# One score matrix in the first scan, attention tiles in pairs, and narrow products prepared ahead, in a two-block kernel on one core

## The chip, the core and the metric

The kernel runs on one core of a Trainium2 chip. The metric is the device time of one execution in microseconds; 2547.91 us is the median of three runs of the kernel before (2546.81 to 2548.03). The engines are TensorE (PE in the profile; PEld is its weight load), VectorE (DVE), ScalarE (ACT), GpSimd (POOL) and SyncE (SP), which issues the large loads. Each works through a queue of its own; they meet in counting semaphores.

## What is computed

Two blocks follow each other on 256 latent tokens of width 1024.

The first block has two layers on 256 latent and 256 context tokens (512 in all):

```python
h = modulate(x, norm1_g[i], shift, scale)          # both streams; shift, scale, gates = silu(c) @ ada_w + ada_b
o = gla_mixer(h) if i == 0 else na_mixer(h)        # gated linear attention, then neighbourhood attention
x = x + g1 * o
x = x + g2 * conv_ffn(modulate(x, norm2_g[i], ...))
```

`gla_mixer`: 4 heads, forward and backward direction, chunks of 64 tokens. In each direction a token attends to itself and to the earlier (later) ones of its chunk with decay, and takes the state of the chunks before. Both directions are added, normalised per head, multiplied by silu(r), transposed and projected. `na_mixer`: 16 heads of 64; 256 latent queries against 512 keys, softmax of scores + bias, times values. `conv_ffn`: two products to 2816 columns (one through a three-tap convolution and silu), their product, and a narrow product back to 1024. The second layer ends with the latent stream only.

The second block is a convolution and scan mixer and a mixture of 64 experts over 256 tokens, whose 400 MB of weights are read whole. The change touches nothing in it.

## The kernel before

The first block keeps activations transposed (features on partitions, 8 chunks of 128). Products of activations with weights are split: weight and activation are each rounded (`..._hi`, on ScalarE) and the rest taken (`..._lo`, on VectorE), and `split_mm` (L519) makes three fp32r products. All large weights come as 88 slabs through four ring slots, issued by SyncE in one fixed order, each when the product that used its slot last is done (`free`); the experts' weights follow in the same queue.

The order on each engine is written out by hand: one function per engine (`@block.tensor`, `scalar`, `vector`, `gpsimd`, `sync`).

First scan (L670 to L745). A step `hd` is one head and direction (even forward, odd backward). On TensorE: `scan_scores` (scores of all chunks into bank 0), `scan_keys` (four transposes, bank 1), `gate_logits(hd + 2)`, `late_turn(hd - 1)`, `scan_updates(hd, 0)`, `late_rows(hd, 0)`, in odd steps from 3 on `y_turn`, `scan_updates(hd, 1)`, the rest of `late_rows`, in odd steps `scan_out`. `late_rows` multiplies a 2 MB slab of the modulation weights each, two or three slabs a step (`ADA_BATCH`); they fill time of the scan. `late_read` (ScalarE) copies the rows, `late_turn` brings the bias and the rows into columns, `late_columns` (ScalarE) stores them. On VectorE a step is `decayed(hd + 1)`, `mask_scores` (predicated copy of bank 0 into `g_att[dr]`), every second time `gated`, `states(hd)` (seven steps of 64x256 to 128x256, the first four behind update 0, the rest behind update 1), `cumulate(hd + 2)`. On ScalarE: `keys_turned`, `late_columns`, `gate_log(hd + 2)`, `y_turned`, `decays(hd + 2)`, `late_read`, `scan_norm`; in step 0 also SiLU over `g_r`. `scan_out(h)` adds, for each of four token tiles, two products of the score matrices with v and up to four with states. Then the projection: six of eight chunks of the first four column groups, `y_turn` of the last head, and the rest with residual and norm sums (L744 to L762).

Feed-forward (`ffn` on each engine). 22 wide units, each of two products of 8 chunks; unit 21 ends the wide part. Then `wo_hi` and `f_lo`: ScalarE rounds the first narrow slab (`ffn_w_out_hi(l, 0)`) and all 22 activation chunks (`f_hi`), VectorE takes the rests. TensorE's eight narrow groups of 22 chunks wait for all of `ffn_act`, for `w_lo` and, in the first group, for each `f_lo`.

Attention (L798 to L834). A tile `i` is one head and 128 queries (h = i // 2). TensorE: scores of tile i + 2, transposes of tile i (four), output of tile i - 1 (four products of 64 columns out). VectorE: score + bias (L2009), maximum (L2011), its negation (L2012), and for the tile before reciprocal and scaling (L2018, L2019). ScalarE: exponential with sum, copy of the transposed tile, copy of the output. Three tiles `n_s`, three score banks. GpSimd waits for the last value product, loads `metaT`, clears `n_bias` and then loads the 32 bias tiles, four ahead.

## Time and profile before

| | us |
|---|---|
| median of 3 runs | 2547.91 |
| the profiled execution | 2554.06 |
| its span, first to last instruction | 2551.8 |
| TensorE busy | 2097.3 (82%) |
| VectorE busy | 912.5 (36%) |
| ScalarE busy | 673.3 (26%) |
| GpSimd busy | 56.0 (2%) |

| stage | from | to |
|---|---|---|
| first modulation slabs, first projections | 0 | 195 |
| first scan | 195 | 341 |
| its projection and norm | 341 | 420 |
| first feed-forward, wide / narrow | 420 / 674 | 669 / 804 |
| q, k, v products of the attention | 814 | 934 |
| attention | 934 | 1037 |
| projection, second feed-forward | 1037 | 1275 |
| second block up to the experts | 1275 | 1600 |
| experts and end | 1600 | 2552 |

A timeline row gives start, length, engine and line, and in brackets how long the engine had been idle before it and what ended that. A single fp32 product has two records on PE (a transpose one), so counts are twice the products; some records are missing. PEclk in the stretch table is the clock granted to TensorE, 1.00 being 2.4 GHz and 0.50 1.2 GHz.

### The profile page before, as it was taken

The numbers are of one execution on the slowest core, as the hardware profiler recorded it, in microseconds if no ns is written. First come the engines' busy times: TensorE is split into PE (matmuls) and PEld (weight loads), VectorE is DVE, ScalarE is ACT, GpSimd is POOL, SyncE is SP. The second block draws the span as 40 slices with busy tenths as digits, with TensorE's granted clock in tenths as the row PEclk, the third lists the DMA queues.
The fourth block names the chain that finished last, engine by engine and source line by source line (L and its number), as shares of the span: only waits on it lengthen the run. The fifth ranks groups of instructions, "written<-read, shape, count | busy, mean of one in ns | idle before, by whom it ended". The sixth has DMA issues, their size and how long they took to land.

```text
span 2551.8 us, 37428 instructions
## 1 busy us (share of the span) xinstructions
PE 2097.3 (82%) x16374; PEld 1521.8 (60%) x16374; DVE 912.5 (36%) x1638; ACT 673.3 (26%) x1173; POOL 56.0 (2%) x81
## 2 busy tenths in 40 slices
PE   6997998999998989999989999666666666666655
PEld 4895755888776875799988445433343343334332
DVE  2335623433423217466475432433311111111112
ACT  4234313323314315455355211111111111111111
POOL 0011100000000011000010000000000000000000
PEclk9998899999998989999999998788888888878888
DMA  7107741222222321153541035599999999999996
GB/s 318 67 34 302 293 179 52 99 99 79 69 101 99 118 98 48 69 184 139 190 168 42 1 155 198 244 426 428 426 427 427 427 425 428 427 427 427 427 427 288
DMA packets 44433, 592.11 MB, mean 232 GB/s; under 512 B 5528, under 2 KB 5717, under 8 KB 8176
## 3 DMA queue, kind: packets, MB, share of 16 engines
q1 hardware_dynamic: 40608, 579.36, 55.5%
q0 software_dynamic: 2880, 8.45, 1.0%
q8 instruction: 131, 2.15, 0.3%
q10 hardware_dynamic: 784, 1.91, 0.2%
q14 instruction: 30, 0.25, 0.0%
HBM read 588.64 MB, written 1.05 MB: 231 GB/s over the span
## 4 chain that ended last, share of the span: by engine, by line
PE 54%; DMA 26%; DVE 4%; ACT 2%; issue 1%; POOL 0%; DVEq 0%; ACTq 0%
DMA s_ring<-in_w_up 10%; PE bank L521 10%; PE bank L523 10%; PE bank L522 10%; DMA s_arena<-in_w_up 8%; PE bank L1091 5%; DMA s_xT<-in_w_up 4%; DMA s_hT<-in_w_up 3%; PE bank L1105 2%; PE bank L1004 1%; PE bank L813 1%; PE bank L803 1%; PE bank L941 1%; PE bank L758 1%; DMA s_arena<-in_w_down 1%
## 5 line engine op out<-in xcount | busy, mean ns | idle before, releaser
L521 PE MATMUL bank<-s_arena_r 128*128 128x256 f32 (+2 forms) x1656 | 544.1, 329 | 36.9 <-DVE s_hT_r L1788 34.5
L1212 ACT ACTIVATE s_arena<-bank 32x256 f32<-32x256 f32 (+6 forms) x455 | 180.1, 403 | 1105.7 <-PE bank L1091 573.6
L523 PE MATMUL bank<-s_arena_r,s_ring_r 128*128 128x512 f32 (+2 forms) x1312 | 442.3, 337 | 0.0
L1091 PE MATMUL bank<-s_ring,s_arena 128*32 128x256 f32 x2048 | 301.3, 506 | 135.8 <-DMA s_xT<-in_w_up 45.7
L522 PE MATMUL bank<-s_hT_r,s_arena_r 128*128 128x512 f32 (+2 forms) x1096 | 369.8, 337 | 0.0
L521 PEld LDWEIGHTS bank<-s_arena_r 128*128 128x128 f32 x1656 | 314.3, 190 | 73.0 <-issue 33.3
L1783 DVE TENSOR_TENSOR s_ring_r<-s_ring,s_arena_r 128x2048 fp32r<-128x2048 f32 (+1 forms) x96 | 232.5, 2425 | 301.6 <-ACT s_arena_r L1212 301.5
L1091 PEld LDWEIGHTS bank<-s_ring,s_arena 128*32 128x32 f32 x2048 | 145.4, 144 | 216.2 <-issue 203.0
L523 PEld LDWEIGHTS bank<-s_arena_r,s_ring_r 128*128 128x128 f32 x1312 | 251.5, 192 | 27.1
L1212 ACT ACTIVATE s_arena_r<-s_ring 128x2048 fp32r<-128x2048 f32 (+1 forms) x96 | 193.2, 2016 | 139.2 <-PE bank L523 138.1
L522 PEld LDWEIGHTS bank<-s_hT_r,s_arena_r 128*128 128x128 f32 x1096 | 210.8, 192 | 21.7
L2331 DVE TENSOR_TENSOR s_arena<-s_arena,bank 64x256 f32<-64x256 f32 x64 | 27.1, 423 | 545.1 <-ACT s_arena L1212 545.1
L1091 PE MATMUL bank<-s_arena 128*32 128x256 f32 x1024 | 128.9, 510 | 83.4 <-DMA s_ring<-in_w_up 36.0
L1091 PEld LDWEIGHTS bank<-s_arena 128*32 128x32 f32 x1024 | 66.2, 145 | 121.0 <-issue 114.5
L1212 ACT ACTIVATE s_arena<-s_arena 128x512 f32<-128x512 f32 (+7 forms) x182 | 92.6, 542 | 166.3 <-DVE s_arena L1776 78.3
L522 PE MATMUL bank<-s_ring_r,s_arena_r 128*128 128x256 f32 (+1 forms) x464 | 130.1, 280 | 0.0
L1091 PE MATMUL bank<-s_xT,s_arena 128*32 128x256 f32 x512 | 91.9, 537 | 37.3 <-DMA s_ring<-in_w_up 37.3
L522 PE MATMUL bank<-s_arena_r 128*128 128x512 f32 (+1 forms) x352 | 120.6, 343 | 0.0
L2387 DVE COPY s_arena<-bank 32x256 f32<-32x256 f32 x128 | 54.3, 424 | 143.4 <-PE bank L1105 141.0
L1091 PE MATMUL bank<-s_hT,s_arena 128*32 128x256 f32 x512 | 84.3, 501 | 16.3 <-DMA s_ring<-in_w_up 16.3
L523 PE MATMUL bank<-s_arena_r,s_hT_r 128*128 128x256 f32 (+1 forms) x336 | 94.3, 281 | 0.0
L1212 ACT ACTIVATE s_arena<-bank,s_cols 128x512 f32<-128x512 f32 (+2 forms) x76 | 48.5, 648 | 161.1 <-PE bank L523 123.7
(318 smaller groups left out, 2795.7 us busy)
## 6 DMA issues: line engine op xcount, KB each, us to landing
s_ring<-in_slabs SPq DMA_DIRECT2D x72, 2048.0 KB, 8.3
s_ring<-in_w_down SPq DMA_DIRECT2D x32, 2048.0 KB, 28.7
s_ring<-in_w_up SPq DMA_DIRECT2D x32, 2048.0 KB, 33.1
s_ring<-in_w_gate SPq DMA_DIRECT2D x32, 2048.0 KB, 33.4
s_arena<-in_w_gate SPq DMA_DIRECT2D x16, 2048.0 KB, 33.1
s_arena<-in_w_up SPq DMA_DIRECT2D x16, 2048.0 KB, 33.9
s_arena<-in_w_down SPq DMA_DIRECT2D x16, 2048.0 KB, 28.7
s_ring<-in_slabs SPq DMA_DIRECT2D x16, 1408.0 KB, 6.3
```

The costliest lines, as they stand in the source:

```text
L521: mm(out, w_hi_, x_hi_, start=start, stop=False)
L522: mm(out, w_hi_, x_lo_, start=False, stop=False)
L523: return mm(out, w_lo_, x_hi_, start=False, stop=stop)
L758: last = mm(pb[m % 4][:, :], w[:, k, 128 * (m % 4):128 * (m % 4) + 128], g_qk[:, 4 * (k % 2) + k // 2, :], start=k == 0, stop=k == DC - 1, ...
L803: mm(NA_BANK[i % 3][:, :], n_q[p0:p0 + 64, h // 2, 128 * qt:128 * qt + 128], n_k[p0:p0 + 64, h // 2, :], start=True, stop=True)\
L813: last = mm(pb[4 + i % 2][p0:p0 + 64, 0:128], n_v[:, k, 64 * h:64 * h + 64], n_pt[:, i % 2, 128 * k:128 * k + 128], start=k == 0, stop=k == 3)
L1091: last = mm(pb[b][32 * q:32 * q + 32, 0:256], x[:, c, :], w[q // 2][:, c, 256 * (q % 2):256 * (q % 2) + 256], start=c == 0, stop=c == DC - ...
L1105: last = mm(pb[3 + b][32 * q:32 * q + 32, 0:256], e_hT[:, b, 64 * a + 32 * half_:64 * a + 32 * half_ + 32], w[:, 2 * half_ + a, 256 * q:25 ...
L1212: return act.activation(out, in_, func, **kw)
L1783: TTn(view_r, view, hi.bitcast(F32), ALU.subtract).then_inc(S["w_lo"], 1)
L2331: return TTn(e_hid[0:64, b, :], e_sg[0:64, b, :], pb[b][64:128, 0:256], ALU.mult)
L2387: dve.tensor_copy(y_g[32 * j:32 * j + 32, g % 2, 256 * q:256 * q + 256], pb[3 + b][32 * q:32 * q + 32, 0:256]).then_inc(S["y_dve"], 1)
```

## The change

- Scan: one matrix `g_att` for both directions. The backward mask leaves the diagonal out; after the backward copy the matrix is multiplied by `g_twice` (2 on the diagonal, 1 elsewhere). `scan_out` makes one score product for each token tile.
- `r` is read from PSUM with SiLU in the same instruction; its second half goes to banks 4 to 7. `scan_scores(0)` waits for four of these reads, and the gate product of step 0 for all eight.
- `late_turn` is made of plain transposes, `late_columns` moves to VectorE (in `states`, before the fifth one) and adds the bias there; `late_read(hd - 1)` comes right after `keys_turned(hd)`. In each step from 1 on `scan_updates(hd, 0)` comes before `late_turn`, and all `late_rows` after the second update.
- Projection behind the scan: five groups ahead instead of four, the last turn after the first and the last y transposes after the third of them.
- Feed-forwards: before unit 21's own work ScalarE rounds the first narrow slab and chunks 0 and 1, VectorE takes their rests; these two have places of their own (`f_hi`). TensorE waits for 20 activations instead of 22, and the narrow groups use banks 2 to 5.
- Attention: tiles in pairs of heads (`na_tile`): tile 2j on partitions 0 to 63, tile 2j + 1 on 64 to 127. Scores come as two products one after the other into two of four banks, outputs as eight products in turn on the two halves of one bank, with one copy. Six logit tiles. Scores are negated while the bias is taken off, the minimum is the bias of an exponential with scale -1. The scores of pairs 0 and 1 are made between the value products, pair 2 right behind, and ScalarE's first four exponentials between its value copies. GpSimd loads metaT and the bias from the end of the first feed-forward on.

```diff
+        n_s = [n_s01[:, 0, :], n_s01[:, 1, :], n_s23[:, 0, :], n_s23[:, 1, :], sq[:, 0, :], sq[:, 1, :]]
+
+        def na_tile(i):
+
+            return 2 * (i // 4) + i % 2, i // 2 % 2
...
-            pool.wait_ge(S["na_v_mm"], 16)
+            pool.wait_ge(S["ffn_out_mm"], DC)
...
+                pool.dma_start(n_bias[:, i % 4, 0:NT], d["na_bias"][h, qt]).then_inc(S[f"na_bias_in{i % 4}"], 16)
...
-                pe.wait_ge(S["ffn_act"], 22 * l + FC)
+                pe.wait_ge(S["ffn_act"], 22 * l + FC - 2)
...
             def late_turn(b):
                 pe.wait_ge(S["ada_row"], ADA_EARLY + b + 1)
-                k, (l, s) = ADA_BATCH[b], divmod(ADA_AT[b], ADA_N)
-                mm(pb[5][:, 3 * P:3 * P + 8 * k], ident, col("ada_b2", 96 * l + 8 * s, 8 * k), start=True, stop=False, skip_group_check=True)
-                for i in range(k):
-                    o = 3 * P + 8 * i
-                    last = mm(pb[5][:, o:o + 8].rearrange("p (j n) -> p j n", n=2), ada_late_sb[:, i, :], ada_sel, start=False, stop=True, skip_group_check=True)
+                for i in range(ADA_BATCH[b]):
+                    last = pe.transpose(pb[5][:, P * i:P * i + P], ada_late_sb[:, i, :], ident)
                 last.then_inc(S["ada_tr"], 1)
...
-                    for dr in range(2):
-                        mm(bank[:, o:o + 256], g_att[:, dr, P * tt:P * tt + P], g_v[:, tt, 256 * h:256 * h + 256], start=dr == 0, stop=False,
-                           skip_group_check=True)
+                    mm(bank[:, o:o + 256], g_att[:, P * tt:P * tt + P], g_v[:, tt, 256 * h:256 * h + 256], start=True, stop=False, skip_group_check=True)
...
                 scan_scores(hd)
                 scan_keys(hd)
+                if hd == 0:
+                    pe.wait_ge(S["gla_r_ev"], 8)
...
                     gate_logits(hd + 2)
+                scan_updates(hd, 0)
                 if hd >= 1:
                     late_turn(hd - 1)
-                scan_updates(hd, 0)
-                late_rows(hd, 0)
+                else:
+                    late_rows(hd, 0)
                 if hd >= 3 and hd % 2:
                     y_turn(hd // 2 - 1)
                 scan_updates(hd, 1)
-                for i in range(1, ADA_BATCH[hd]):
+                for i in range(0 if hd else 1, ADA_BATCH[hd]):
                     late_rows(hd, i)
                 if hd % 2:
                     scan_out(hd // 2)
-            late_turn(7)
-            w = got(FIRST["gla_out"])
-            for m in range(4):
+            for m in range(GLA_AHEAD):
+                w = got(FIRST["gla_out"] + m // 4)
                 for k in range(6):
-                    mm(pb[m][:, :], w[:, k, 128 * m:128 * m + 128], g_qk[:, 4 * (k % 2) + k // 2, :], start=k == 0, stop=False, skip_group_check=True)
-            y_turn(HEADS - 1)
+                    mm(pb[m][:, :], w[:, k, 128 * (m % 4):128 * (m % 4) + 128], g_qk[:, 4 * (k % 2) + k // 2, :], start=k == 0, stop=False,
+                       skip_group_check=True)
+                if m == 0:
+                    late_turn(7)
+                if m == 2:
+                    y_turn(HEADS - 1)
             pe.wait_ge(S["gla_y_ev"], 2 * HEADS)
...
+            def na_scores(j):
+                for a in range(2):
+                    i = 2 * j + a
+                    h, qt = na_tile(i)
+                    if i >= 4:
+                        pe.wait_ge(S["na_add"], i - 3)
+                    mm(NA_BANK[i % 4][:, :], n_q[64 * a:64 * a + 64, h // 2, 128 * qt:128 * qt + 128], n_k[64 * a:64 * a + 64, h // 2, :],
+                       start=True, stop=True).then_inc(S["na_s_mm"], 1)
+
+            def na_out(j):
+                pe.wait_ge(S["na_pt"], 2 * j + 2)
+                if j >= 2:
+                    pe.wait_ge(S["na_o_ev"], j - 1)
+                for k in range(4):
+                    for a in range(2):
+                        i = 2 * j + a
+                        h, qt = na_tile(i)
+                        last = mm(pb[j % 2][64 * a:64 * a + 64, 0:128], n_v[:, k, 64 * h:64 * h + 64], n_pt[:, i % 4, 128 * k:128 * k + 128],
+                                  start=k == 0, stop=k == 3, skip_group_check=True)
+                last.then_inc(S["na_o_mm"], 1)
...
+                if k in (8, 9):
+                    na_scores(k - 8)
+            na_scores(2)
...
+            for j in range(NA_H):
+                for a in range(2):
+                    i = 2 * j + a
+                    pe.wait_ge(S["na_p"], i + 1)
+                    if i >= 2:
+                        pe.wait_ge(S["na_pt"], i - 1)
+                    for k in range(4):
+                        last = pe.transpose(pb[2 + a][:, 128 * k:128 * k + 128], n_s[i % 6][:, 128 * k:128 * k + 128], ident)
+                    last.then_inc(S["na_tr"], 1)
+                if j >= 1:
+                    na_out(j - 1)
+                if j + 3 < NA_H:
+                    na_scores(j + 3)
...
-                ffn_w_out_hi(l, 0)
                 act.wait_ge(S["ffn_in_mm"], 44 * (l + 1))
-                act.wait_ge(S["ffn_act"], 22 * (l + 1))
-                for c in range(FC):
+                for c in range(2, FC):
+                    act.wait_ge(S["ffn_act"], 22 * l + (c + 1 if c < DC + 2 else FC))
                     A(f_hi(c, T), f_act[:, c, 0:T], ACT.Copy).then_inc(S["f_hi"], 1)
...
+                    if i == FC - 1:
+                        ffn_w_out_hi(l, 0)
+                        for c in range(2):
+                            A(f_hi(c, T), f_act[:, c, 0:T], ACT.Copy).then_inc(S["f_hi"], 1)
...
-                    copy("gla_r_mm", 8 * s + 4 + u + 1, "gla_r_ev", pb[u][:, :], g_r[:, u, 512 * s:512 * s + 512])
+                    copy("gla_r_mm", 8 * s + 4 + u + 1, "gla_r_ev", pb[4 * s + u][:, :], g_r[:, u, 512 * s:512 * s + 512], func=ACT.Silu)
...
+            r_read(0)
             r_read(1)
+            tables(LOG_EXP)
             for hd in range(8):
                 keys_turned(hd)
                 if hd >= 1:
-                    late_columns(hd - 1)
+                    late_read(hd - 1)
                 if hd + 2 < 8:
...
-                if hd == 0:
-                    act.wait_ge(S["gla_r_ev"], 8)
-                    for u in range(4):
-                        A(g_r[:, u, :], g_r[:, u, :], ACT.Silu).then_inc(S["gla_r_ev"], 1)
-                late_read(hd)
...
+            late_read(7)
...
-                A(n_s[:, i % 3, :], n_s[:, i % 3, :], ACT.Exp, bias=n_mx[:, i % 3, 1:2], accum_out=n_rs[:, i % 3, 0:1]).then_inc(S["na_exp"], 1)
...
+                A(n_s[i % 6], n_s[i % 6], ACT.Exp, scale=-1.0, bias=n_mx[:, i % 6, 0:1], accum_out=n_rs[:, i % 6, 0:1]).then_inc(S["na_exp"], 1)
+
+            def na_read(j):
+                act.wait_ge(S["na_o_mm"], j + 1)
+                h, qt = na_tile(2 * j)
+                A(n_o[:, h // 2, 128 * qt:128 * qt + 128], pb[j % 2][:, 0:128], ACT.Copy).then_inc(S["na_o_ev"], 1)
+            for k in (10, 11):
+                half_hi(k, "na", NA_DONE)
+            for u in range(8):
+                if u >= 4:
+                    na_exp(u - 4)
+                copy("na_v_mm", 8 * (u // 4) + 4 + u % 4 + 1, "na_v_ev", pb[u % 4][:, :], n_v[:, u % 4, 512 * (u // 4):512 * (u // 4) + 512])
...
+                if i % 2 == 0 and i >= 2:
+                    for a in range(2):
+                        if i + 2 + a < 2 * NA_H:
+                            na_exp(i + 2 + a)
...
+                if i >= 2 and i % 2 == 0:
+                    na_read(i // 2 - 1)
+            na_read(NA_H - 1)
...
+                def act_rest(c):
+                    dve.wait_ge(S["f_hi"], FC * l + c + 1)
+                    TTn(f_lo[:, c, 0:T], f_act[:, c, 0:T], f_hi(c, T).bitcast(F32), ALU.subtract).then_inc(S["f_lo"], 1)
...
+                    if i == FC - 1:
+                        ffn_w_out_lo(l, 0)
+                        for c in range(2):
+                            act_rest(c)
...
-                ffn_w_out_lo(l, 0)
-                for c in range(FC):
-                    dve.wait_ge(S["f_hi"], FC * l + c + 1)
-                    TTn(f_lo[:, c, 0:T], f_act[:, c, 0:T], f_hi(c, T).bitcast(F32), ALU.subtract).then_inc(S["f_lo"], 1)
+                for c in range(2, FC):
+                    act_rest(c)
...
+                att = g_att.rearrange("p (a n) -> p a n", n=P)
+                if dr:
+                    dve.wait_ge(S["att_cp"], hd)
+                last = dve.copy_predicated(att, in_chunk[dr].bitcast(U32).unsqueeze(1).to_broadcast([P, 4, P]), pb[0][:, :].rearrange("p (a n) -> p a n", n=P))
+                if dr:
+                    step(last)
+                    last = TTn(att, att, g_twice.unsqueeze(1).to_broadcast([P, 4, P]), ALU.mult)
+                last.then_inc(S["att_cp"], 1)
...
+            def late_columns(b):
+                k, (l, s) = ADA_BATCH[b], divmod(ADA_AT[b], ADA_N)
+                dve.wait_ge(S["ada_tr"], ADA_EARLY + b + 1)
+                TTn(mod[:, l, 4 * s:4 * s + 4 * k, :], pb[5][:, 0:P * k].rearrange("p (j n) -> p j n", n=32)[:, :, 0:2],
+                    col("ada_b2", 96 * l + 8 * s, 8 * k).rearrange("p (j n) -> p j n", n=2), ALU.add).then_inc(S["ada_late"], 1)
...
+                    if i == 4 and hd >= 1:
+                        late_columns(hd - 1)
...
-                TTn(n_s[:, i % 3, :], NA_BANK[i % 3][:, :], n_bias[:, i % 4, :], ALU.add).then_inc(S["na_add"], 1)
+                if i >= 6:
+                    dve.wait_ge(S["na_tr"], i - 5)
+                STT(out=n_s[i % 6], in0=NA_BANK[i % 4][:, :], scalar=-1.0, in1=n_bias[:, i % 4, :], op0=ALU.mult, op1=ALU.subtract).then_inc(S["na_add"], 1)
...
-                step(dve.tensor_reduce(n_mx[:, i % 3, 0:1], n_s[:, i % 3, :], AX_X, ALU.max))
-                TS(n_mx[:, i % 3, 1:2], n_mx[:, i % 3, 0:1], -1.0, None, ALU.mult).then_inc(S["na_max"], 1)
...
+                dve.tensor_reduce(n_mx[:, i % 6, 0:1], n_s[i % 6], AX_X, ALU.min).then_inc(S["na_max"], 1)
...
+            for k in range(1, 11):
+                half_lo(k, "na")
+            for i in range(2):
+                na_add(i)
+            half_lo(11, "na")
+            for i in range(2, 4):
+                na_add(i)
+            for j in range(NA_H):
+                for a in range(2):
+                    na_share(2 * j + a)
+                if j + 2 < NA_H:
+                    for a in range(2):
+                        na_add(2 * j + 4 + a)
```

## Rows read from the trace of the kernel before

**Rows 1.** Stretch table: us; busy PE, PEld, DVE, ACT, POOL; PEclk, DMA share, GB/s
```profile
1700.00:2500.00 800.00, 522.11 (x5828) 304.55 (x5820) 168.79 (x454) 86.83 (x243) 0.00 (x0) 0.83 1.01 427
```

**Rows 2.** Timeline of PE in the scan: start us, us, engine, line, instruction, count
```profile
227.62 1.13 PE L713 MATMUL bank<-s_arena 128*128 128x256 f32 x4
...
239.00 0.40 PE L598 MATMUL bank<-s_cols,s_ka 128*128 128x24 f32 x2
...
239.99 1.13 PE L702 MATMUL bank<-s_arena 64*128 64x256 f32 x8
```

**Rows 3.** Waits of PE in 195:341: waited for, us in total, times, longest
```profile
PE bank L598 <- ACT s_arena L1212: 15.0, 3, 9.1
PE bank L702 <- DVE s_arena L1943: 0.8, 3, 0.3
```

**Rows 4.** Timeline of ACT in steps 0 and 1 of the scan
```profile
208.71 2.91 ACT L1212 ACTIVATE s_arena<-s_arena 128x512 f32<-128x512 f32 x7 [8.54 <-DVE s_arena L1908]
...
212.93 3.90 ACT L1212 ACTIVATE s_ring<-s_ring 128x1024 f32<-128x1024 f32 x4
```

**Rows 5.** Stretch table in the scan and at the first narrow group
```profile
280.00:285.00 5.00, 5.00 (x99) 4.23 (x95) 2.35 (x6) 0.73 (x2) 0.00 (x0) 0.69 0.31 59
...
673.60:680.00 6.40, 6.35 (x17) 5.04 (x18) 6.40 (x11) 6.40 (x14) 0.00 (x0) 0.58 0.15 58
```

**Rows 6.** Timeline of PE in the projection behind the scan
```profile
364.40 3.70 PE L758 MATMUL bank<-s_arena,s_ring 128*128 128x512 f32 x8 [1.36 <-ACT s_arena L1212]
372.18 2.07 PE L506 MATMUL bank<-s_sq,s_ones 128*128 128x512 f32 x2 [4.08 <-ACT s_sq L1212]
```

**Rows 7.** Timelines at the joint of the first feed-forward: PE, DVE, ACT
```profile
673.65 0.76 PE L521 MATMUL bank<-s_hT_r,s_arena_r 128*128 128x512 f32 x1 [4.55 <-DVE s_arena_r L1820]
...
664.36 0.75 DVE L1775 SCALAR_TENSOR_TENSOR s_arena<-bank,s_cols,s_arena 128x510 f32<-128x510 f32 x1 [5.64 <-ACT s_arena L1212]
...
669.99 4.27 ACT L1212 ACTIVATE s_hT_r<-s_arena 128x512 fp32r<-128x512 f32 x8 [0.98 <-DVE s_arena L1816]
...
691.71 2.56 ACT L1212 ACTIVATE s_arena_r<-s_ring 128x2816 fp32r<-128x2816 f32 x1 [7.72 <-PE bank L523]
```

**Rows 8.** Timelines at the joint of the second feed-forward: ACT, DVE
```profile
1208.93 2.54 ACT L1212 ACTIVATE s_arena_r<-s_ring 128x2816 fp32r<-128x2816 f32 x1
...
1212.71 3.09 DVE L1783 TENSOR_TENSOR s_ring_r<-s_ring,s_arena_r 128x2816 fp32r<-128x2816 f32 x1
```

**Rows 9.** Timeline of PE in the attention: its start, and one tile
```profile
946.77 1.11 PE L825 MATMUL bank<-s_ka,s_arena 128*128 128x128 f32 x4 [10.23 <-DVE s_arena L2019]
...
963.58 0.66 PE L825 MATMUL bank<-s_ka,s_arena 128*128 128x128 f32 x4
964.16 1.09 PE L813 MATMUL bank<-s_arena 128*64 128x128 f32 x8
965.18 1.12 PE L803 MATMUL bank<-s_arena 64*128 64x512 f32 x2
```

**Rows 10.** Stretch table in the attention
```profile
946.80:962.00 15.20, 15.20 (x44) 8.71 (x45) 8.17 (x20) 5.21 (x14) 2.15 (x4) 0.50 0.10 32
962.00:1034.00 72.00, 71.32 (x381) 42.17 (x379) 54.95 (x133) 44.02 (x108) 11.82 (x22) 1.00 0.15 43
```

**Rows 11.** Timelines at the start of the attention: POOL, DVE
```profile
937.40 2.16 POOL L463 DMA_DIRECT2D s_arena<-in_na_bias  x4 [0.31 <-POOL s_arena L458]
...
943.00 0.69 DVE L2009 TENSOR_TENSOR s_arena<-bank,s_arena 128x512 f32<-128x512 f32 x1 [38.70 <-DMA s_arena<-in_na_bias]
...
946.04 0.15 DVE L2018 RECIPROCAL s_arena<-s_arena 128x1 f32<-128x1 f32 x1
...
946.63 0.68 DVE L2009 TENSOR_TENSOR s_arena<-bank,s_arena 128x512 f32<-128x512 f32 x1
```

**Rows 12.** Timeline of PE in the second block's scan: 64-column outputs in alternating halves
```profile
1413.67 0.66 PE L922 MATMUL bank<-s_arena 128*64 128x128 f32 x8
1414.26 0.71 PE L918 MATMUL bank<-s_arena 128*128 128x128 f32 x4
```

More of the change, by code:

```diff
@@ L634, in _, with token_major @@
             pe.wait_ge(S["gla_qk_ev"], 8)
-            def token_major(k, name, freed, after):
+            def token_major(k, name, freed, after, first=0):
                 wh, wl = g_w_hi[k % 2 + (2 if k >= 8 else 0)], half(place_r[FIRST["gla"] + k // 2], k % 2)
@@ L685, in scan_keys @@
                     pe.wait_ge(S["kd_cp"], hd)
-                else:
-                    pe.wait_ge(S["gla_r_ev"], 8)
                 pe.wait_ge(S["late_decayed"], 2 * hd + 2)
@@ L754, in _ @@
                 w = got(FIRST["gla_out"] + m // 4)
-                if m >= 4:
-                    pe.wait_ge(S["proj_x"], 2 * (m - 3))
-                for k in range(6 if m < 4 else 0, DC):
-                    last = mm(pb[m % 4][:, :], w[:, k, 128 * (m % 4):128 * (m % 4) + 128], g_qk[:, 4 * (k % 2) + k // 2, :], start=k == 0, stop=k == DC - 1,
+                if m >= GLA_AHEAD:
+                    pe.wait_ge(S["proj_x"], 2 * (m - GLA_AHEAD + 1))
+                for k in range(6 if m < GLA_AHEAD else 0, DC):
+                    last = mm(pb[m % GLA_AHEAD][:, :], w[:, k, 128 * (m % 4):128 * (m % 4) + 128], g_qk[:, 4 * (k % 2) + k // 2, :], start=k == 0, stop=k == DC - 1,
                               skip_group_check=True)
@@ L1999, in _ @@
                 h_rest(2, c, hT[:, c, :], hT_r[:, c, :], h_hi[:, c, :])
-            for k in range(1, 12):
-                half_lo(k, "na")
             def na_add(i):
```

120 lines of the change are left out of this document (35 added, 85 removed).

## Prediction

> **What bounds the kernel now.** I read the stretch table first. From 1700 to 2500 us the 16 DMA engines are full at 427 GB/s [rows 1]: the expert stage, bound by its weights. Nothing in the diff touches it, and its loads stand in SyncE's queue behind semaphores of the work before it, so time won before it moves it forward whole. The change lies in four places ahead of it: the first scan (195 to 341 us) with the projection behind it (to 413), the joint between wide and narrow products in each feed-forward (669 and 1200), and the attention (934 to 1037). There I looked in the order of time for rows in which TensorE sat idle, and for what ended them; where it isn't idle, only an instruction less helps.
>
> **1. The scan and the projection after it.** TensorE's scan work is one queue, so an instruction less counts in full, as long as the chain beside it (states on VectorE, decays on ScalarE, turned keys) doesn't end later.
> - One score matrix: the two products of a token tile take 1.13, or 1.06 without what overlaps the next [rows 2], 0.53 each; 16 of 32 go: -8.5. The price, a 128x512 multiply of 0.69 (as L2009, [rows 11]) in each backward head, stands on VectorE ahead of the states, while the updates they need are still to come: 0, and without that cover +2.8.
> - Late columns: the bias product and three selections take 239.00 to 239.99 [rows 2]; four transposes take 0.58 [rows 9], three 0.45. About 0.5 for each of seven turns in the scan: -3.5.
> - SiLU moved ahead: in head 1 TensorE waits 9.1 for ScalarE [rows 3], which ends its decays at 211.6, loads a table and runs four SiLUs to 216.8 before its copies [rows 4]. The SiLUs now replace the copies of r from PSUM, under the projection. What ends last then is the key copy (0.6) behind the decays, at 212.2; the wait runs from 208.0 to 212.3: -4.9. The table load held ScalarE for 1.3 (211.6 to 212.93, [rows 4]). The Trainium skill ("ScalarE: Activation LUTs", What ACT_TABLE_LOAD costs) counts 2.66 us for a switch of sets; by it this gain would be an estimated 1.4 larger, but the next ACTIVATE started after 1.3.
> - Updates no longer stand behind the turn, and all slabs of a batch follow the second update. In heads 3 and 5 the wait of 2.95 ((15.0 - 9.1) / 2, [rows 3]) falls to about 1.4, since one slab more (1.9) lies between the update that starts the chain and the wait, and the key copy (0.6) ends it and not the slab copy: -3.1. Heads 6 and 7 have no gate product left as cover: +1.9.
> - New waits: 2.15 us of states lie between the two updates, today covered by a slab's products (wait 0.3, [rows 3]). Now only the turn (0.3 to 0.45) stands there, in heads 3, 5, 7 also 1.0 of y transposes. Seven waits, of 1.35 to 1.7 and of 0.5 to 0.7, 7.8 in all, less 0.8 of today: +7.0.
> Sum -11.1. The clock: it is 0.69 at 280 to 285 [rows 5], behind a stretch without any wait, of 16-row and 8-column products and transposes. Two long waits go with the slow stretch behind them (-3); the new short waits thin the sparse stretches, and a dip can fall on any head: +1 to +8, I take +4. Scan -10.1 (-4 to -15). Slabs: 4.9 us each at 427 GB/s, three in 15, against heads of 12 to 19; one wait of 1, within this range.
> - Projection: TensorE waits 1.36 for the y copies and 4.08 for a square, which stands behind both engines' splitting of the next weights, and then runs at half clock (2.07 for a chunk of 1.02) [rows 6]. From the transposes' end (363.0) to the square 9.1 us pass. Now two groups of 5.2 (364.4's eight records are four products in 3.5, so 0.87 each, six a group) stand between: -7.6 with the turn's 0.45 (-5.6 if 2 us stick out).
> Together -17.7.
>
> **2. First feed-forward.** TensorE stops 4.55 [rows 7] for the split of the first narrow weights (2.54, 3.09, [rows 8]) and of the activations. Its first group runs from 673.65 to 691.71 (when ScalarE's wait for it ends), 18.05, of which 6.4 at a mean clock of 0.58 [rows 5]: 2.7 lost, 15.4 of work. Now the weight split (released when unit 20 ends, about 658) and chunks 0 and 1 lie under unit 21, whose convolution wants VectorE at 664.4 and gets it at 664.9; its result waits for 669.1 anyway. TensorE goes on at 669.1, waits 0.2 at chunk 2 and ends at 684.7. The second weight: ScalarE 20 x 0.53 from 669.1, then 2.54, makes 682.3; VectorE's 3.09 end at 685.3. The second group starts at 685.3 instead of 691.7: -6.4 (-4 if the clock dips there all the same).
>
> **3. Second feed-forward.** A unit lasts only 5.7 us, too short for 2.54 + 3.09. VectorE takes the last convolution only at 1201.3, the last SiLU ends at 1202.8, and ScalarE, then with 20 chunks, is at the second weight at 1208.9, as today [rows 8]. VectorE ends its part at 1214.6 instead of 1215.8, and the second group starts at least as much earlier, 1.2. But TensorE, done with the first group at 1210.7, waits 3.9 there and may pay 1.7 of half clock: -1 (-2 to +1).
>
> **4. Attention.** Start: TensorE idles 10.23 [rows 9], because the bias is asked for after the last value product: GpSimd issues from 937.40, the first sum starts at 943.00 [rows 11]. The loads now go out when the first feed-forward ends (GpSimd has nothing else queued between), and four tiles pass sum, maximum and exponential under the value products. After the stall TensorE is at clock 0.50 for 15.2 us [rows 10]; that goes too.
> Steady state: a tile takes TensorE transposes 0.58, outputs 1.02, scores 1.05 (1.12 less overlap), 2.65 in all, without a gap [rows 9]. A pair: scores 1.06, both halves of the rows at once (four 64-row products of 256 columns take 1.06 in [rows 2], 0.27 each, against 0.53 with 128 rows); transposes 1.16; outputs 16 records at the pace of 64-column outputs in alternating halves (eight in 0.59, [rows 12]): 1.18, or 2.04 if they don't overlap. Sum 3.4. VectorE: sum and negation in one operation, 0.75 (as L1775, PSUM and a scalar column, [rows 7]) + 0.03; minimum 0.62 (a pass over the same tile, priced as the sum's 0.69 of [rows 11] less overlap); reciprocal and scaling 0.59 (946.04 to 946.63, [rows 11]): 1.99 a tile, 3.98 a pair. ScalarE: exponentials 2 x 0.8, copies 2 x 0.53, 0.3: 3.0. VectorE becomes the bound, at 3.98 against 5.3.
> Time: the value products end at 933.9 and now carry two score pairs, 936.0; a third, 937.1. Thirteen periods and the last two sums (2.8) end at 991.7. Behind them scalings, transposes, outputs and copies of two pairs, no longer overlapped, 8.7: the projection starts at 1000.4 instead of 1036.9: -36.5. Bounds: outputs 1.5 a pair, -35.5; scores not overlapped, -27.5; fused sum 0.87, -33; 1.9 a tile, -39.
>
> **Sum.** -17.7 - 6.4 - 1 - 36.5 = -61.6. The profiled execution took 2554.06 (span 2551.8), 6.2 over the median of 2547.9: from its own time 2492.5, from the median 2486.3.
>
> **Rivals.** A: the halves don't overlap in the attention. TensorE needs 2.1 + 1.16 + 2.04 = 5.3 a pair as today, and only the start is won, -14.6: 2508. For it: no attention product has been issued this way; against it the two rows above. B: the clock. Every pair gets a wait of 0.6, and transposes are a third of the rest. At 1.2 GHz a pair costs 6.8, 16 pairs 109 us, 13 more than today instead of 36.5 less: 2535. Against it: 962 to 1034 ran at 1.00 with transposes a fifth of the time; for it, TensorE was busy for 15 us at 0.50 before that [rows 10]. The Trainium skill ("TensorE: Matmul & The Clock Gate", Part 4: PE-mode transpose) says that transposes don't count as busy for the clock, which speaks for B. C, slower: the same in the scan too, whose new waits follow updates and transposes. Its work is about 118 us, and what of it runs at half clock costs its own length again. On top of B the change loses from 12.5 us of it on; with a third of it (40) the time is 2575.
>
> **Chances.** Forecast 0.84, A 0.08, B 0.04, C 0.04. The parts' bounds give -40 to -70 for the forecast, 2478 to 2508, which takes A in; below I leave 4 more for clock dips outside the scan that may go too: 2474 to 2508. A measurement here tells 0.2% (5 us) from no change. Faster 0.95 (A and B with it), same 0.01 (C just past its point, or a part that I have not seen), slower 0.04.
>
> **What would show it.** Head 1's wait 4 to 5 us, for keys; waits of 1.5 for states in heads 2, 4, 6; no wait over 1 before the first squares of the projection; in the first feed-forward the second narrow group 16 us after the last wide product, in the second a wait of nearly 4; none for the bias; a pair each 4.0 us with VectorE without gaps. A pair at 5.3 with TensorE full is A; PEclk under 0.8 in the attention is B. I am wrong on the whole if the experts' first load doesn't come earlier by what TensorE won.

## The result and the profile after

The changed kernel takes 2490.4 us (median of five, 2488.4 to 2493.25) against 2548.03 of the kernel before, beside it on the same chip: ratio 0.977, 95% interval 0.9756 to 0.9784. The profiled execution took 2492.72 (span 2490.9); a second set of five runs gave 2489.59. The forecast was 2486, for the profiled execution 2492.5.

The stages, from the first and last product of each in the two TensorE timelines (us):

| stretch | before | after | difference | forecast |
|---|---|---|---|---|
| first scan, to the last product of `scan_out` | 195.0 to 340.7 | 195.1 to 334.6 | -6.2 | -10.1 |
| projection and norm, to the first wide product | to 420.1 | to 406.3 | -7.7 | -7.6 |
| first feed-forward and norm, to q | to 814.0 | to 793.9 | -6.3 | -6.4 |
| q, k, v and attention, to its projection | to 1036.9 | to 977.8 | -39.0 | -36.5 |
| projection, second feed-forward, norm | to 1285.3 | to 1226.9 | +0.7 | -1 |
| all behind it | to 2551.8 | to 2490.9 | -2.5 | 0 |

The last row holds nothing of the change: it is how one execution differs from another (in the twelve profiles taken later this part was 1262 to 1268 us long). The spans differ by 60.9, the medians by 57.6: the profiled execution of before was 6.0 above its median, that of after 2.3.

**Attention.** TensorE, one pair; the row answers to [rows 9]:

```profile
936.17 1.25 PE L840 MATMUL bank<-s_ka,s_sq 128*128 128x128 f32 x8 [0.49 <-DVE s_sq L2045]
937.35 1.09 PE L814 MATMUL bank<-s_arena 128*64 128x128 f32 x16
938.37 1.13 PE L803 MATMUL bank<-s_arena 64*128 64x512 f32 x4
939.99 1.25 PE L840 MATMUL bank<-s_ka,s_arena 128*128 128x128 f32 x8 [0.49 <-DVE s_arena L2045]
```

From one pair's first transpose to the next 3.82 us pass, for what took 5.3 before, and each pair begins behind a wait of 0.49 for VectorE's scaling. The outputs of both tiles together take 1.02 (937.35 to 938.37), what those of one took in [rows 9]. VectorE in the same pair has no gap:

```profile
936.62 0.68 DVE L2038 SCALAR_TENSOR_TENSOR s_arena<-bank,s_arena 128x512 f32<-128x512 f32 x1
937.34 0.69 DVE L2040 TENSOR_REDUCE s_arena<-s_arena 128x1 f32<-128x512 f32 x1
937.94 0.68 DVE L2038 SCALAR_TENSOR_TENSOR s_arena<-bank,s_arena 128x512 f32<-128x512 f32 x1
938.66 0.69 DVE L2040 TENSOR_REDUCE s_arena<-s_arena 128x1 f32<-128x512 f32 x1
939.26 0.15 DVE L2044 RECIPROCAL s_arena<-s_arena 128x1 f32<-128x1 f32 x1
939.45 0.48 DVE L2045 TENSOR_SCALAR s_arena<-s_arena 128x512 f32<-128x512 f32 x1
939.85 0.15 DVE L2044 RECIPROCAL s_arena<-s_arena 128x1 f32<-128x1 f32 x1
```

A tile costs it 0.72 + 0.60 + 0.59 (start to start), a pair 3.82. The stretch table of after, for the scan, the attention and the second joint (columns as in [rows 1]):

```profile
195.00:334.60 139.60, 119.43 (x1818) 84.55 (x1816) 84.68 (x153) 47.59 (x113) 17.11 (x12) 0.91 0.80 322
930.00:965.00 35.00, 30.60 (x268) 18.50 (x264) 33.74 (x74) 24.85 (x63) 9.62 (x18) 1.00 0.23 68
1156.00:1166.00 10.00, 9.92 (x69) 9.68 (x69) 3.42 (x3) 1.08 (x3) 0.00 (x0) 0.83 0.18 74
```

The attention runs at clock 1.00 in spite of a wait in each pair and although transposes are a third of TensorE's work in it.

**Scan.** TensorE's waits in after (as [rows 3]), and two lines of its timeline:

```profile
PE bank L710 <- DVE s_arena L1974: 8.6, 7, 1.8
PE bank L710 <- ACT s_arena L1229: 7.2, 4, 4.2
PE bank L586 <- DMA s_ring<-in_slabs: 4.3, 3, 2.9
```

```profile
212.27 2.08 PE L710 MATMUL bank<-s_arena 64*128 64x256 f32 x8 [4.20 <-ACT s_arena L1229]
...
261.89 2.52 PE L586 MATMUL bank<-s_ring,s_arena 128*32 128x128 f32 x64 [2.93 <-DMA s_ring<-in_slabs]
```

Before, TensorE was busy for 128.4 of 145.7 us and waited 17.1; now it is busy for 119.4 and waits 20.1. So the scan has 9.0 less of busy time, in which work and clock are mixed, and 3.0 more of waits. The 4.2 is head 1's wait for keys (9.1 before), the 8.6 are the new waits for states, the 4.3 those for slabs (0.6 before).

**Joints.** In the first feed-forward the second narrow group starts 16.2 us after the end of the last wide product (655.3), with a short wait (the first row). In the second feed-forward the first narrow group has waits of 0.6 and 1.5, and the second group starts behind one of 3.6 (the second row):

```profile
671.45 0.50 PE L532 MATMUL bank<-s_arena_r 128*128 128x512 f32 x1 [0.59 <-DVE s_ring_r L1793]
```

```profile
1156.08 0.38 PE L532 MATMUL bank<-s_arena_r 128*128 128x256 f32 x1 [3.61 <-DVE s_ring_r L1793]
```

### The profile page after: what moved, and what is told of

Its sections match the earlier page's. It is cut to its first block, busy times and chain, and to the rows that moved or that the text cites. A ratio compares the mean times of both kernels' runs of the same rounds, so it can differ in the third digit from the quotient of the medians.

```text
span 2490.9 us, 37228 instructions
## 1 busy us (share of the span) xinstructions
PE 2046.5 (82%) x16306; PEld 1491.1 (60%) x16306; DVE 909.0 (36%) x1619; ACT 660.9 (27%) x1145; POOL 57.4 (2%) x81
## 3 DMA queue, kind: packets, MB, share of 16 engines
HBM read 588.64 MB, written 1.05 MB: 237 GB/s over the span
## 4 chain that ended last, share of the span: by engine, by line
PE 51%; DMA 26%; DVE 5%; ACT 3%; issue 2%; SPq 0%; DVEq 0%; ACTq 0%
DMA s_ring<-in_w_up 12%; PE bank L532 10%; PE bank L534 10%; PE bank L533 10%; DMA s_arena<-in_w_up 8%; PE bank L1108 5%; DMA s_xT<-in_w_up 4%; DMA s_hT<-in_w_up 3%; PE bank L1122 2%; PE bank L1021 1%; PE bank L958 1%; PE bank L770 1%; PE bank L575 1%; PE bank L1095 1%; PE bank L758 1%
## 5 line engine op out<-in xcount | busy, mean ns | idle before, releaser
L1229 ACT ACTIVATE s_arena<-bank 32x256 f32<-32x256 f32 (+7 forms) x439 | 173.7, 408 | 1086.1 <-PE bank L1108 573.8
L1108 PEld LDWEIGHTS bank<-s_ring,s_arena 128*32 128x32 f32 x2048 | 150.7, 145 | 213.0 <-issue 198.9
L1229 ACT ACTIVATE s_arena<-s_arena 128x512 f32<-128x512 f32 (+8 forms) x172 | 85.4, 532 | 157.3 <-DVE s_arena L1786 77.6
L1108 PE MATMUL bank<-s_xT,s_arena 128*32 128x256 f32 x512 | 89.7, 528 | 37.4 <-DMA s_ring<-in_w_up 37.4
L533 PEld LDWEIGHTS bank<-s_ring_r,s_arena_r 128*128 128x128 f32 (+1 forms) x464 | 85.9, 185 | 0.5
```

Of the source, the lines that this page charges most:

```text
L533: mm(out, w_hi_, x_lo_, start=False, stop=False)
L1108: last = mm(pb[b][32 * q:32 * q + 32, 0:256], x[:, c, :], w[q // 2][:, c, 256 * (q % 2):256 * (q % 2) + 256], start=c == 0, stop=c == DC - ...
L1229: return act.activation(out, in_, func, **kw)
```

## Experiments

Each kernel was timed beside the kernel before, whose medians in these sets were 2547.8 to 2549.1. Differences "to the changed kernel" are taken from its first median, 2490.4; its second, 2489.59, shows that one of a microsecond or two means nothing. "Attention" is the stretch from the end of the last value product to the first product of the attention's projection: 103.0 before, 61.4 in the changed kernel. Not undone by themselves were the SiLUs, the turns by transposes, the update ahead of the turn, and the projection's groups ahead; what they are worth is read from profiles of the whole scan alone.

**The attention as it was, all else changed** (`attention_old`): the hunks of the attention reversed.

> The changed kernel with the attention of the kernel before (tiles one by one, three logit tiles, bias loaded after the last value product); scan, projection and both feed-forwards stay changed. Theory (the parts add up): in the two profiles the stretch from the end of the value products to the first product of the attention's projection took 103.0 us before (933.9 to 1036.9) and 63.6 after (914.2 to 977.8, the two early score pairs taken off), so this kernel is 39.4 slower than the changed one, about 2530, 18 under the kernel before. Rival (part of that gain belongs to what stands around it, by the clock): a difference of under 30 or over 45.

2527.5 us, 37.1 over the changed kernel; attention 98.0, 36.6 longer. The parts add up: the forecast of 39.4 was 2 too high. The 5 us under the 103.0 of before are the clock behind the stall: half speed lasted some 6 us there, not 15 as in [rows 10]:

```profile
923.50:932.00 8.50, 8.50 (x32) 5.05 (x32) 5.37 (x12) 3.66 (x10) 1.48 (x3) 0.66 0.14 44
932.00:940.00 8.00, 8.00 (x44) 4.68 (x42) 6.29 (x16) 4.94 (x12) 1.64 (x4) 1.00 0.17 51
```

Half the difference in time at half speed, (15.2 - 6) / 2, is 4.6. So a part of the 39.0 between the two first profiles is the clock of that one execution; the medians say 37.

**The early start undone** (`bias_late`):

```diff
-            pool.wait_ge(S["ffn_out_mm"], DC)
+            pool.wait_ge(S["na_v_mm"], 16)
...
+            for i in range(4):
+                na_exp(i)
```

(with the sums behind the last weight split).

> The changed kernel with the early start of the attention undone: GpSimd asks for metaT and the bias after the last value product, all sums stand behind the last weight split and the first four exponentials behind the value copies. The pairs stay. Theory (VectorE sets the pace, so what it had done ahead is lost on top of the stall): the first sum starts 9.1 us after the products' end as in the kernel before, the four sums done ahead cost 4 x 1.32 more: +14 to the changed kernel, up to +20 if TensorE is at half clock behind the stall. Rival (VectorE has slack and catches up): +9 at most.

2507.5 us (+17.1); attention 75.6 (+14.2). TensorE's third score pair waits for the first sum, its first transposes start at 931.5:

```profile
926.09 3.39 PE L803 MATMUL bank<-s_arena 64*128 64x512 f32 x4 [9.56 <-DVE s_arena L2038]
931.45 1.94 PE L840 MATMUL bank<-s_ka,s_arena 128*128 128x128 f32 x8 [1.97 <-DVE s_arena L2045]
```

VectorE has no slack to catch up with: the theory stands. Of the attention's gain over `attention_old` the early start has 14.2 by the stretches and the pairs 22.4; by the medians it is 17.1 and 20.0.

**Outputs one half after the other** (`out_in_turn`):

```diff
-                for k in range(4):
-                    for a in range(2):
+                for a in range(2):
+                    for k in range(4):
```

> The changed kernel with only the order of the eight output products of a pair changed: first the four of one half of the columns, then the four of the other, instead of in turn. Theory (halves overlap only where neighbours in the queue use different halves): the eight take 2.05 us instead of 1.09, TensorE then needs 4.3 a pair against VectorE's 3.82, and 14 pairs cost 0.5 each: +7. Rival (the order is of no account, a product of 64 columns out costs half by itself): pair 3.82, +0.

2492.8 us (+2.4); attention 62.8 (+1.4). The pair stays at 3.82, the rival's number, but not for the rival's reason:

```profile
939.83 1.25 PE L840 MATMUL bank<-s_ka,s_arena 128*128 128x128 f32 x8
941.01 1.58 PE L814 MATMUL bank<-s_arena 128*64 128x128 f32 x16
942.52 1.13 PE L803 MATMUL bank<-s_arena 64*128 64x512 f32 x4
```

The outputs take 1.51 instead of 1.02: the order counts, but by half of what the theory expected, and these 0.49 just fill TensorE's wait of 0.49.

**No scaling** (`no_scaling`): the scaling `TS(n_s[i % 6], ...)` is left out, and one of a single column stands in its place.

> The changed kernel without the scaling of the attention's probabilities by their sums (a one-column operation stands in its place, so the output isn't the attention's). It takes 0.3 to 0.35 us a tile from VectorE. Theory (VectorE's 3.82 a pair is the pace): its pair falls to 3.2, TensorE's 3.3 becomes the pace, 14 pairs win 0.45 each: -6. Rival (a loop of latencies through exponential, scaling, transposes and copy sets the pace and not VectorE's work): pair 3.7 or more, -2 at most.

2483.6 us (-6.8); attention 53.6 (-7.8), pair 3.2, and between 918 and 960 TensorE waits twice in all (1.8 us). VectorE's work was the pace, and what comes next, TensorE at 3.2, is 0.6 a pair away. That is more than the wait of 0.49: the transposes of a pair take 1.02 here and 1.18 in the changed kernel (936.17 to 937.35). Probably the other 0.15 is a wait for the second tile's scaling inside that row; no view shows it apart.

**Slabs spread otherwise** (`slabs_even`):

```diff
-ADA_BATCH = [2, 3, 3, 3, 3, 2, 2, 2]
+ADA_BATCH = [2, 3, 3, 2, 3, 3, 2, 2]
```

> The changed kernel with one number changed: the slabs of late rows are spread 2, 3, 3, 2, 3, 3, 2, 2 over the heads instead of 2, 3, 3, 3, 3, 2, 2, 2. In the profiles of the changed kernel and its variants so far TensorE waits 2.3 to 5.0 us for slabs, most of it for the third slab of head 3 (2.9 at 261.9). Theory (all slabs behind the second update give their ring slots back late, and head 3 asks for three right after): with two in head 3 that wait goes, and three in head 5 cover the 1.0 that head 6 waits for its keys: 3 to 5 us faster than the changed kernel, the scan 134 us long instead of 136 to 139.5. Rival (the waits for slabs lie where the chain of decays would make TensorE wait anyway): the same time comes up as a wait for keys in head 4, less than 1 us won.

2490.3 us, scan 139.4. The theory falls, and not to the rival: the wait went from head 3's third slab to head 5's:

```profile
295.95 1.96 PE L586 MATMUL bank<-s_ring,s_arena 128*32 128x128 f32 x64 [2.93 <-DMA s_ring<-in_slabs]
```

Waits for slabs are 5.0 in all. In the profiles with the changed scan as it is they are 2.3 to 5.0, so the sums don't tell these kernels apart; the place of the long wait does.

**A slab back between the updates** (`slab_between`):

```diff
-                else:
-                    late_rows(hd, 0)
+                late_rows(hd, 0)
...
-                for i in range(0 if hd else 1, ADA_BATCH[hd]):
+                for i in range(1, ADA_BATCH[hd]):
...
-                    if i == 4 and hd >= 1:
+                    if i == 1 and hd >= 1:
```

The first update stays ahead of `late_turn`, so this takes back one part of the reordering only.

> The changed kernel with the first slab of every head put back between the two updates (behind late_turn), as in the kernel before, and late_columns moved to stand behind the first state so that bank 5 is free for it. Theory (the chain from the second update over states, sums, decays to the next turned keys is what paces the heads; a slab behind the update hides it, one ahead of it delays it): the waits for states fall from 8.6 us to some 3, those for slabs to about 1, but waits for keys in heads 3 to 7 grow by 2 us or more each: 1 to 5 us slower than the changed kernel. Rival (a slab covers the same wherever it stands): faster by the 5.6 of the states and 3 of the slabs.

2489.8 us, scan 136.2. Its waits:

```profile
PE bank L710 <- ACT s_arena L1228: 13.7, 5, 4.2
PE bank L586 <- DVE s_mod L1955: 2.0, 7, 0.3
PE bank L586 <- DMA s_ring<-in_slabs: 0.6, 1, 0.6
PE bank L710 <- DVE s_arena L1973: 0.3, 1, 0.3
```

States and slabs are hardly waited for any more (0.3 and 0.6), but keys 3.05 in heads 3 and 5 each and 2.76 in head 6. It is 16.6 in all, against 20.1 (19.8 in the repeated profile). In time (-0.6) the two places of the slab can't be told apart: both expectations were off, slower by 1 to 5 and faster by 8.6.

**Score products twice** (`scores_twice`): the loop `for dr in range(2)` put back around the one product.

> The changed kernel with each product of the score matrix with the values issued twice (so the scan's output isn't the reference's), VectorE's work as in the changed kernel. Theory (TensorE's queue is the bound of the scan, an instruction less counts in full): 16 products of 0.53 more, 8.5, less up to 1 us by which the keys of the following head are waited for less: +7.5 to +8.5 to the changed kernel. Rival (the chain beside TensorE sets the heads' pace, the products were hidden): +3 or less.

2499.4 us (+9.0); in the profile TensorE is busy for 124.7 in the scan and the scan takes 143.0. The profiles with the changed scan as it is have 116.3 to 120.4 of busy time and a length of 135.6 to 140.3. So the one profile shows 4 to 8 more of busy time and 3 to 7 more of length, and the medians all of the 8.5. The rival's 3 or less is out; that a product less counts in full rests on the medians.

**The second preparation undone** (`ffn1_old`): the prepared splits are back behind unit 21 for l = 1. "Stretch" is from the first wide product of this feed-forward to the first product of the next block.

> The changed kernel with the preparation undone in the second feed-forward alone (no split of narrow weights and of chunks 0 and 1 ahead of unit 21). Stretch from the first wide product to the end of the narrow part and norm (to the next wide product): 211.3 us in the kernel before, 212.1 in the changed one, where TensorE waits 3.6 for the second weight split and the group behind it lasts 9.6 instead of 7.7 us. Theory (the wait and the half clock behind it give back all that the early start wins): 0.8 us faster than the changed kernel, 211.3 for the stretch. Rival (the preparation pays here too, what is lost is the luck of one profile): slower by 1 to 2.

2494.1 us (+3.7); stretch 213.2. The undoing was not exact: I put the first weight split behind one wait more than it had before, and TensorE waits 6.2 where it waited 5.3. The other profiles show why no single one decides: with the preparation in place the stretch is 209.4 to 209.5 (`slabs_even`, `bias_late`, `joined_alternate`) or 211.5 to 212.1 (the rest). About half of this difference lies behind the wait for the second weight split. In `slabs_even`:

```profile
1141.00:1156.00 15.00, 10.87 (x75) 10.29 (x74) 12.35 (x28) 11.55 (x23) 0.00 (x0) 0.89 0.41 127
1156.00:1166.00 10.00, 10.00 (x82) 9.52 (x81) 3.41 (x3) 3.37 (x3) 0.00 (x0) 1.00 0.41 137
```

There the lower clock falls into the first group, ahead of a wait that takes it up (2.1 instead of 3.6); in after it falls behind the wait (0.83 above), where it costs time. This is 1.5 of the 2.7; the other 1.2 lie in the wide products, which the preparation doesn't touch. So I compare from the end of the last wide product to the first sum of squares behind the second group: 23.5 before, 24.4 in `ffn1_old` (23.5 without the 0.9 of its longer wait), 23.3 in after and 21.8 in `slabs_even`. The preparation is worth 0 to 1.7, by where the dip falls. The medians' 3.7, less 0.9, is more than that, but two medians can differ by a microsecond or two without any change.

**Halves apart, and the first preparation undone** (`apart_ffn0_old`): `na_scores` issues one half ahead of `na_out` and one behind, outputs as in `out_in_turn`; for l = 0 the splits are back behind unit 21.

> The changed kernel with two edits undone in two stages, read apart by their stretches. Attention: the two score products of a pair are put apart (one ahead of the outputs, one behind) and the outputs one half after the other, so that no halves stand next to each other in turn; the amount of work is the same. Theory (halves run at once only as neighbours in the queue): scores 2.1 instead of 1.06, outputs 1.5 instead of 1.02, so TensorE needs 3.33 + 1.0 + 0.49 = 4.8 a pair and is the pace: 14 x 1.0 = +14 in the stretch from the last value product to the projection (61.4). Rival (VectorE hides half of it, or the hardware lets them overlap across other products): +5 or less. First feed-forward: its preparation is undone, units and narrow products as before. Theory: from the last wide product to the start of the second narrow group 22.6 us instead of 16.2, +6.4. Together +20.

2510.6 us (+20.2). Attention 71.9 (+10.5 instead of 14):

```profile
952.17 1.09 PE L840 MATMUL bank<-s_ka,s_arena 128*128 128x128 f32 x8
953.19 1.12 PE L803 MATMUL bank<-s_arena 64*128 64x512 f32 x2
954.24 1.58 PE L814 MATMUL bank<-s_arena 128*64 128x128 f32 x16
```

A score product alone takes 1.05 (953.19 to 954.24), as long as two next to each other; the pair is 4.63 (952.17 to 956.80), with TensorE full. First feed-forward and norm take 395.8 instead of 387.7, +8.1. Here too the split stood behind one wait more (TensorE waits 6.5 instead of 4.55 in [rows 7]); without it +6.2, if that wait counts in full.

**A better version** (`joined_alternate`), with another spread of the slabs as well:

```diff
+ADA_BATCH = [3, 2, 3, 2, 3, 2, 3, 2]
...
+                    dve.tensor_reduce(n_mx[:, p:p + 2, 0:1], src[:, :, :], AX_X, ALU.min)
...
+                dve.reciprocal(n_rs[:, p:p + 2, 1:2], n_rs[:, p:p + 2, 0:1])
...
+                    A(n_s[(i + 1) % 6], n_s[(i + 1) % 6], ACT.Copy, scale=n_rs[:, (i + 1) % 6, 1:2])
```

> The changed kernel with two edits in two stages, read apart by their stretches. Attention: one minimum and one reciprocal for both tiles of a pair, and the scaling of the second tile on ScalarE. Theory (VectorE's 3.82 a pair is the pace, ScalarE at 2.7 has room): VectorE falls to 3.82 - 0.40 (scaling) - 0.19 (reciprocal) - 0.1 (a start saved) = 3.1, and the pace becomes TensorE's 3.2, as in the kernel without scaling: the stretch from the last value product to the projection 61.4 - 7.8 = 53.6. Rival (the way round over ScalarE and back is too long): 3.4 or more a pair, -5 at most. Scan: slabs spread 3, 2, 3, 2, 3, 2, 3, 2 over the heads. Theory (what makes TensorE wait 2.9 is a third slab in an odd head behind an even head of three, wherever it stands): waits for slabs in the scan fall from 4.3 to 2 at most and the scan is 2 us shorter than in kernels with the same order so far (135.6 to 140.4). Rival (as with the other spread, the waits come up elsewhere): 136 to 140. Together -9 to the changed kernel.

2482.55 us (2481.46 to 2487.41), 7.9 and 7.0 under the two medians of the changed kernel; ratio to before 0.9735, interval 0.9716 to 0.9754. Attention 54.5 (-6.9), pair 3.2:

```profile
920.00:960.00 40.00, 38.72 (x351) 24.55 (x346) 37.38 (x61) 39.20 (x99) 11.31 (x22) 1.00 0.28 90
```

Now ScalarE (39.2 of 40), TensorE (38.7) and VectorE (37.4) are all nearly full. The gain is the attention's. The scan took 136.8, within the 135.6 to 140.3 of the other order, and its waits for slabs were 6.5, 4.0 of them for the third slab of head 0, in the place of head 1's wait for keys: the forecast of 2 at most failed.

**The same with odd heads as before** (`joined_odd`): slabs 2, 3, 3, 2, 3, 2, 3, 2, the first one between the updates in odd heads.

> The attention of joined_alternate (joined minimum and reciprocal, scaling of the second tile on ScalarE; 6.9 less from the last value product to the projection than the changed kernel) with another order of the scan: slabs 2, 3, 3, 2, 3, 2, 3, 2, and in the odd heads the first slab stands between the updates, behind late_turn, with late_columns behind the first state; even heads as in the changed kernel. Theory (chain: in an odd head scan_out's 7.5 us cover what the second update starts, so a slab may stand ahead of it; in an even head it may not): waits for states fall by the odd heads' 3.9 to 5, waits for slabs stay under 2, waits for keys as in the changed kernel or 1 more; the sum of waits in the scan 12 to 14 instead of 16.6 to 20.4, 3 us under joined_alternate: 2479. Rival (any order only moves the waits about): the sum stays 16 or more, 2482 to 2484.

2483.1 us (6.5 under the changed kernel beside it), scan 137.5, waits 19.0: 5.2 for states, 9.3 for keys, 3.7 for slabs, 0.8 for the columns. The rival holds.

**The changed kernel again** (`changed_again`).

> The changed kernel once more, beside joined_odd on the same chip, as the measure for it and to see how far the changed kernel's own stretches move from one profile to the next. Expected: 2488 to 2493; the scan 135.6 to 140.4 long, its busy time 116 to 120, its waits 18 to 20.4; second feed-forward 209.4 or 212.1.

2489.59 us; scan 139.7, busy 120.4, waits 19.8; second feed-forward 211.7.

## Why the prediction was right, point by point

- **The sum**: -61.6 forecast, -57.6 by the medians, -61.3 between the two profiled executions. That the profiled execution was met to 0.2 us (2492.5 for 2492.72) is in part luck: the scan won 3.9 less and the second feed-forward 1.7 less than forecast, the attention won 2.5 more, and 2.5 came at the end from no change at all. The forecast from the median, 2486.3, was 4.1 too low. It took from the median what I had read in one execution some 6 above it, and in that execution the half speed behind the attention's stall lasted 15.2 us, in `attention_old` about 6, 4.6 us less lost. If the median execution of before is like the latter, this alone makes up the 4.1; there is one profile of before only, so that isn't shown.
- **What bounds the kernel**: the experts start earlier by what was won. Their first load was issued 60.0 us earlier (before, then after), the 16 DMA engines are full at 427 GB/s as before (1640 to 2440 us), and the two profiles differ by 58.4 at the end of the second feed-forward and by 60.9 at the end:

```profile
1478.93 0.43 SPq L418 DMA_DIRECT2D s_arena<-in_w_gate  x1
```

```profile
1418.88 0.43 SPq L428 DMA_DIRECT2D s_arena<-in_w_gate  x1
```

- **Head 1's wait**: 4.3 forecast, 4.20. Decays end at 211.7 and the key copies start at 211.64, with no table load between. Before, the load has a row of its own there, and the SiLUs started right behind it (212.93):

```profile
211.63 1.28 ACT L1205 ACT_TABLE_LOAD   x1
```

The gain is 4.9 as the sum by the trace said; the larger one by the Trainium skill ("ScalarE: Activation LUTs", What ACT_TABLE_LOAD costs) isn't seen.
- **Keys in heads 3 and 5**: 5.9 to 1.3, -4.6 instead of -3.1 (head 5 waits 1.3 as forecast, head 3 not at all; its waits for slabs come later in the head). Heads 6 and 7: +1.0 instead of +1.9. **States**: +7.8 (8.6 less 0.8) instead of +7.0.
- **Slabs**: the term that was wrong. One wait of 1 was forecast; there are three, 4.3 in all for 0.6 before, +3.7. I compared the rate of the loads with the length of the heads and left out when the ring slots come free: all of head 2's three slabs are used together at its end, and three more are wanted some 8 us later. `slabs_even` shows the wait of 2.9 moving with the third slab of an odd head, and in `slab_between`, where the first slab of a head is used earlier, it is gone. That the free slots are the reason is argued from this, not shown.
- **Work and clock in the scan**: -11.0 forecast (-8.5, -3.5, +1 of clock), -9.0 in the first profile, -8.0 to -12.1 in those of all kernels with the same scan; which of it is the clock and which the instructions wasn't separated. The scan as a whole, -6.2, lies in the range of -4 to -15, as do the others with this scan (135.6 to 140.3 long, -5.4 to -10.1).
- **The order of the updates** was costed at +5.8 of waits net. `slab_between` takes back one part of it, the place of the first slab: waits fall by 3.5 and the time by nothing that can be measured. The other part, the first update ahead of the turn, was never undone. Since the new order adds waits (+4.2: states and keys but for head 1's), the scan's gain must come from fewer products, the SiLUs and the turns; of these only the products were tested (`scores_twice`).
- **Projection**: -7.7 for -7.6; the first norm sum (364.99) starts without a wait.
- **First joint**: 16.2 us for 16.2, and 6.2 on undoing it.
- **Second joint**: the second group starts 14.0 after the last wide product (1142.1) instead of 15.9, where at least 1.2 earlier was forecast. But behind the wait of 3.6 the clock falls (0.83 above), and the group takes 9.6 instead of 7.7, so nothing is won. I had named 1.7 for that and took less; the stage's +0.7 is within the range, and the loss falls away in some executions.
- **Attention**: 3.82 a pair for 3.98 (sum and negation in one 0.72 instead of 0.78, minimum 0.60 instead of 0.62), which over 14 pairs is 2 of the 2.5 us by which the stage was better. `no_scaling` and `joined_alternate` show that VectorE was the pace: with less work on it the pair falls to 3.2, in the second of them although the second tile's scaling goes by way of ScalarE there.
- **Rival A**: its condition doesn't hold, since both halves take 1.02. Its price was too high: where they are really apart (`apart_ffn0_old`), the pair is 4.63 and not 5.3, mostly because outputs one half after the other cost 1.51 and not 2.04. **Rivals B and C**: the clock is 1.00 in the attention with a wait in each pair; the Trainium skill's sentence on transposes ("TensorE: Matmul & The Clock Gate", Part 4: PE-mode transpose) may hold: whether transposes alone would lower the clock no run here shows, and with them a third of the work it stayed up. The scan's mean clock is 0.91, as before.

## What to carry to other kernels

Where one engine becomes the pace of a loop, add up the next engine's time as well. The distance between the two is both what the second may lose for nothing (TensorE lost 0.49 a pair in `out_in_turn`) and the most that relief of the first can win (0.6 in `no_scaling`). A wait moved is not a wait removed: before reordering work that covers waits, list every chain it covers, the return of buffers included. A load's wait is found from when its slot comes free and not from the mean rate.

## What the runs showed that I had not expected

- The 64-column outputs of two tiles, four products each in the two halves of the columns, take 1.02 in turn and 1.51 one half after the other, and those of one tile took 1.02 in [rows 9]. So a part of the overlap is there even without taking turns.
- The second feed-forward, with the same instructions in kernels that differ elsewhere, is up to 2.7 us longer in some profiles than in others; 1.5 of this is whether the lower clock falls ahead of a wait or behind it. And the busy time of one unchanged scan goes from 116.3 to 120.4 us.
